# A hybrid encoder layer on one core: last projection granule and logits by token tile, a shorter reciprocal root, second low parts split around the first ranks, and the facts' casts on GpSimd

## The reference

```python
def prep(x, pos, g_norm1, w_in, b_forget, g_fox_q, g_fox_k, g_mem_q):
    h = rmsnorm(x, g_norm1)
    z = h @ w_in
    rq, rk, rv, rg, fq, fk, fv, ff, mq, gl = jnp.split(z, SPLIT_POINTS, axis=-1)
    fq = rmsnorm(heads(fq, H_F, D_F), g_fox_q)
    fk = rmsnorm(heads(fk, H_F, D_F), g_fox_k)
    mq = rmsnorm(heads(mq, H_M, D_M), g_mem_q)
    ...
def merge_and_ffn(...):
    merged = (gates[..., 0, :] * (o_r @ w_br_ret) + gates[..., 1, :] * (o_f @ w_br_fox)
              + gates[..., 2, :] * (o_m @ w_br_mem))
    x = x + merged @ w_out
    return x + hier_moe(rmsnorm(x, g_norm2), ...)
def hier_moe(h, w_rg, b_rg, w_re, b_re, w_g, w_u, w_d):
    lg = t @ w_rg + b_rg                        # 4 groups: the best one is taken
    le = t @ w_re + b_re                        # 8 experts of that group: the best two
    ...
    for g in range(N_GROUPS):                   # 32 experts, 1024 -> 256 -> 1024
        a = jnp.einsum('td,edf->tef', t, w_g[g]); u = jnp.einsum('td,edf->tef', t, w_u[g])
        out = out + jnp.einsum('tef,efd->td', jax.nn.silu(a) * u * comb[:, g, :, None], w_d[g])
```

## Time and profile before

| | |
|---|---|
| median of 3 runs | 659.27 us (658.0 to 659.7) |
| the profiled execution | 657.81 us |
| its span, first to last instruction | 656.0 us |
| PE busy | 630.8 us (96%) |
| DVE, ACT, POOL busy | 348.1, 255.8, 125.7 us |
| granted TensorE clock, mean | 0.998 |
| HBM | 167.48 MB read, 9.06 MB written |

### The profile page before, as it was taken

How to read it: one execution, slowest core, us unless ns; L and a number is a source line. 1 busy time by engine, 2 the same in 40 slices (tenths; PEclk the granted TensorE clock), 3 DMA queues, 4 the chain that set the end, 5 groups by cost and what they waited for, 6 DMA issues and landing times.

```text
span 656.0 us, 9434 instructions
## 1 busy us (share of the span) xinstructions
PE 630.8 (96%) x3509; PEld 422.0 (64%) x3509; DVE 348.1 (53%) x745; ACT 255.8 (39%) x487; POOL 125.7 (19%) x139
## 2 busy tenths in 40 slices
PE   5999999998999999999999999999999999999995
PEld 3887888877888776778777878763434444344431
DVE  4649347995357566744446855565533334234312
ACT  5673343346334455664953334332321222131200
POOL 0017525664000411010000010012301311210301
PEclk9999999999999999999999999999999999999999
DMA  8975432354222833203867989499999999999993
GB/s 304 423 272 186 146 130 92 125 204 182 78 84 97 295 131 129 98 33 129 325 223 291 427 321 373 142 386 351 425 428 424 428 426 425 425 425 428 427 419 116
DMA packets 36096, 176.67 MB, mean 269 GB/s; under 512 B 4256, under 2 KB 4528, under 8 KB 23632
## 3 DMA queue, kind: packets, MB, share of 16 engines
q1 hardware_dynamic: 33072, 164.87, 63.9%
q0 software_dynamic: 2976, 11.16, 4.8%
HBM read 167.48 MB, written 9.06 MB: 269 GB/s over the span
## 4 chain that ended last, share of the span: by engine, by line
PE 74%; issue 9%; SPq 5%; ACT 4%; DMA 4%; DVE 2%; POOL 0%; POOLq 0%; ACTq 0%; DVEq 0%
PE banks L1696 13%; PE banks L1698 13%; PE banks L1697 13%; PE banks L2070 12%; PE banks L2100 6%; SPq L836 5%; DMA piece<-in_wexp 4%; PE banks L2054 2%; PE banks L2110 1%; ACT z L1130 1%; PE banks L1899 1%; ACT w_hi L1010 1%; PE banks L1978 1%; PE banks L1865 1%; PE banks L1872 1%
## 5 line engine op out<-in xcount | busy, mean ns | idle before, releaser
L1250 DVE TENSOR_TENSOR w_lo<-raw,w_hi 128x1024 fp32r<-128x1024 f32 (+1 forms) x81 | 128.2, 1594 | 74.3 <-ACT w_hi L1010 71.2
L1696 PE MATMUL banks<-w_hi,hT_hi 128*128 128x512 f32 x312 | 124.7, 400 | 2.4 <-ACT z L1037 1.7
L1698 PE MATMUL banks<-w_hi,hT_lo 128*128 128x512 f32 x312 | 121.8, 391 | 0.0
L1697 PE MATMUL banks<-w_lo,hT_hi 128*128 128x512 f32 x312 | 121.6, 390 | 0.0
L1010 ACT ACTIVATE w_hi<-raw 128x1024 fp32r<-128x1024 f32 x79 | 83.5, 1057 | 90.8 <-PE banks L1698 87.1
L2070 PE MATMUL banks<-piece,xs 128*64 128x512 f32 x512 | 114.7, 593 | 0.5 <-DMA piece<-in_wexp 0.5
L2070 PEld LDWEIGHTS banks<-piece,xs 128*64 128x64 f32 x512 | 38.3, 137 | 72.8 <-issue 70.2
L1696 PEld LDWEIGHTS banks<-w_hi,hT_hi 128*128 128x128 f32 x312 | 58.6, 188 | 15.6 <-issue 2.9
L1698 PEld LDWEIGHTS banks<-w_hi,hT_lo 128*128 128x128 f32 x312 | 58.6, 188 | 12.7
L1697 PEld LDWEIGHTS banks<-w_lo,hT_hi 128*128 128x128 f32 x312 | 58.7, 188 | 11.3
L2100 PE MATMUL banks<-piece,act_T 128*64 128x512 f32 x256 | 58.5, 599 | 0.1
(11 more groups left out here) (353 smaller groups left out, 951.2 us busy)
## 6 DMA issues: line engine op xcount, KB each, us to landing
piece<-in_wexp SPq DMA_DIRECT2D x90, 1024.0 KB, 18.8
raw<-in_wstream SPq DMA_DIRECT2D x79, 512.0 KB, 4.3
piece<-in_wexp SPq DMA_DIRECT2D x12, 512.0 KB, 20.7
foxc<-in_foxc POOLq DMA_DIRECT2D x8, 512.0 KB, 4.5
memv<-in_memc SPq DMA_DIRECT2D x8, 512.0 KB, 5.8
memk<-in_memc SPq DMA_DIRECT2D x8, 512.0 KB, 5.9
xT<-in_xT SPq DMA_DIRECT2D x1, 1536.0 KB, 11.3
xtok<-in_xtok SPq DMA_DIRECT2D x1, 1536.0 KB, 7.9
```

The source lines that it names most:

```text
L1250: dve.tensor_tensor(w_lo[:, i % PART_SLOTS, cols], raw[:, i % RAW_SLOTS, cols], w_hi[:, i % PART_SLOTS, cols].bitcast(F32), ALU.subtract). ...
L1696: mm(out, xh, wh, start=start, stop=False, skip_group_check=True)
L1697: mm(out, xh, wl, start=False, stop=False, skip_group_check=True)
L1698: return mm(out, xl, wh, start=False, stop=stop, skip_group_check=True)
```

## The change

1. The last granule of the second output chunk runs tile by tile, 6 matmuls each: both halves `kk` of tile 0, then tile 1, then tile 2. Before, each half went over the three tiles.
2. Tiles 0 and 1 of the transposed `x2` are brought out first (128x256), and tile 2 separately from banks 0 and 1 (128x128). ACT squares tile 2 between the two. The second logits run over tiles 0 and 1 first, then tile 2.
3. `rsqrt` takes one step of a third-order form with 4 instructions and one Newton step of 3 in place of three Newton steps: 9 instructions in place of 11, at every call. `norm2` loses another one, since the squares are now scaled on ACT.
4. `second_low` is cut in two: `second_whole(t)` (the fp32 matmul) and `second_low(t)` (minus `x_hi`). `second_whole(1)` stands before the first ranks, and `second_whole(0)` no longer waits for `x_hi`.
5. The three instructions for the facts of token row and `rstd2` go from DVE's `route_group` to GpSimd.
6. On DVE the first `compact_low` stands after the slots and no longer before them.

```diff
     step("compact", 0, 1, 1)
+    plain("slots", 0)
     s.append(("compact_low", 0, 0, 0, None))
-    plain("slots", 0)
...
-            for step in range(3):
-                chain(dve.tensor_tensor(tmp, out, out, ALU.mult))
-                chain(dve.scalar_tensor_tensor(tmp, tmp, -0.5, x, ALU.mult, ALU.mult))
-                ins = dve.scalar_tensor_tensor(out, tmp, 1.5, out, ALU.add, ALU.mult)
-                if step < 2:
-                    chain(ins)
+            chain(dve.tensor_tensor(tmp, out, out, ALU.mult))
+            chain(dve.tensor_tensor(tmp, tmp, x, ALU.mult))
+            chain(dve.scalar_tensor_tensor(tmp, tmp, -10.0 / 3.0, tmp, ALU.add, ALU.mult))
+            chain(dve.scalar_tensor_tensor(out, tmp, 5.0, out, ALU.add, ALU.mult))
+            chain(dve.tensor_tensor(tmp, out, out, ALU.mult))
+            chain(dve.scalar_tensor_tensor(tmp, tmp, -0.5 * 0.375 ** 3, x, ALU.mult, ALU.mult))
+            ins = dve.scalar_tensor_tensor(out, tmp, 0.5625, out, ALU.add, ALU.mult)
             return ins
...
-            dve.wait_ge(x2t_lg_ready, KT + 1)
+            dve.wait_ge(x2t_lg_ready, KT + 5)
...
-            dve.tensor_copy(info_parts[:, :, 4, 0], cst2("token_row"))
-            chain(dve.tensor_copy(info_parts[:, :, 5, 0], rstd2))
-            dve.tensor_tensor(info_parts[:, :, 5, 1], rstd2, info_parts[:, :, 5, 0].bitcast(F32), ALU.subtract).then_inc(info_in, 1)
...
+        def last_turned(j):
+
+            return ps[:, j % 2, P * (j // 2 - 2):P * (j // 2 - 1)]
+
+        def squares(act, i, t):
+
+            act.wait_ge(x2_ready, T * i + t + 1)
+            if 3 * i + t:
+                act.wait_ge(ss2_ready, 3 * i + t)
+            act.activation(sq_scratch[:, :], x2[:, t, 512 * i:512 * i + 512], ACT.Square, scale=D ** -0.5, accum_out=ss2[:, 3 * i + t:3 * i + t + 1]).then_inc(ss2_ready, 1)
...
+                    for t in range(T - i):
+                        squares(act, i, t)
                 elif kind == "turn_x2":
+                    n = TOK - P * i
                     for j in range(4 * i + 1, 4 * i + 4, 2):
                         act.wait_ge(x2t_lg_ready, j + 1)
-                        act.activation(h2T[:, j, :], ps[:, TURN_BANK[j], 0:TOK], ACT.Copy, scale=gk[:, 16 + j:17 + j]).then_inc(x2t_odd, 1)
+                        act.activation(h2T[:, j, 0:n], ps[:, TURN_BANK[j], 0:n], ACT.Copy, scale=gk[:, 16 + j:17 + j]).then_inc(x2t_odd, 1)
+                    if i:
+                        squares(act, 1, T - 1)
+                        for j in (5, 7):
+                            act.wait_ge(x2t_lg_ready, KT + 4)
+                            act.activation(h2T[:, j, n:TOK], last_turned(j), ACT.Copy, scale=gk[:, 16 + j:17 + j]).then_inc(x2t_odd, 1)
...
+                    if i:
+                        for j in (4, 6):
+                            dve.wait_ge(x2t_lg_ready, KT + 3)
+                            dve.tensor_scalar(h2T[:, j, n:TOK], last_turned(j), gk[:, 16 + j:17 + j], None, ALU.mult).then_inc(x2t_even, 1)
                 elif kind == "norm2":
                     dve.wait_ge(ss2_ready, 2 * T)
-                    chain(dve.tensor_tensor(ss2[:, 0:T], ss2[:, 0:T], ss2[:, T:2 * T], ALU.add))
-                    chain(dve.tensor_scalar(ss2[:, 0:T], ss2[:, 0:T], 1.0 / D, EPS, ALU.mult, ALU.add))
+                    chain(dve.scalar_tensor_tensor(ss2[:, 0:T], ss2[:, 0:T], EPS, ss2[:, T:2 * T], ALU.add, ALU.add))
...
+                elif kind == "route":
+                    pool.wait_ge(rstd2_ready, 1)
+                    pool.tensor_copy(info_parts[:, :, 4, 0], cst2("token_row"))
+                    chain(pool.tensor_copy(info_parts[:, :, 5, 0], rstd2))
+                    pool.tensor_tensor(info_parts[:, :, 5, 1], rstd2, info_parts[:, :, 5, 0].bitcast(F32), ALU.subtract).then_inc(info_in, 1)
...
+            def second_whole(t):
+
+                pe.wait_ge(x2_ready, T + t + 1)
+                mm(ps[:, t, :], ident, x2[:, t, 512:1024], start=True, stop=False, skip_group_check=True)
+
             def second_low(t):
 
                 pe.wait_ge(xhi_ready, T + t + 1)
-                mm(ps[:, t, :], ident, x2[:, t, 512:1024], start=True, stop=False, skip_group_check=True)
                 mm(ps[:, t, :], neg_ident[:, :], x_hi[1][t][:, :], start=False, stop=True, skip_group_check=True).then_inc(xlo_psum, 1)
...
-                    for kk in ((0,) if kind == "k" else (1,)) if i in halved else range(2):
+                    halves = ((0,) if kind == "k" else (1,)) if i in halved else range(2)
+                    for kk, tiles in product(halves, (range(nt),)) if i < NGRAN - 1 else [(h, (t,)) for t in range(nt) for h in halves]:
...
+                                to = ps[:, TURN_BANK[j], t * P:(t + 1) * P] if t < T - 1 else last_turned(j)
+                                ins = nc.tensor.transpose(to, x2[:, t, j * P:(j + 1) * P], ident)
+                                if t:
                                     ins.then_inc(x2t_lg_ready, 1)
                 elif kind == "logits":
                     pe.wait_ge(s_route_in, 32)
-                    for k in range(4 * i, 4 * i + 4):
-                        pe.wait_ge(x2t_odd if k % 2 else x2t_even, k // 2 + 1)
-                        for t in range(T):
+                    for tiles in ((range(T),) if i == 0 else ((0, 1), (2,))):
+                        for k, t in product(range(4 * i, 4 * i + 4), tiles):
+                            pe.wait_ge(x2t_odd if k % 2 else x2t_even, k // 2 + (3 if i and t == T - 1 else 1))
...
                 elif kind == "x_parts" and i == 1:
+                    second_whole(0)
                     second_low(0)
                 elif kind == "route":
+                    second_whole(1)
                     token_ranks(0, 32, 4, [T * NR + 4 * t for t in range(T)])
                     second_low(1)
+                    second_whole(2)
                     second_low(2)
```

More of the change, by code:

```diff
@@ L20 @@
 from contextlib import ExitStack
+from itertools import product
 import numpy as np
@@ L1136, in _ @@
                     act.wait_ge(u_oe, NGROUP)
-                    for t in range(T):
-                        act.wait_ge(x2_ready, T * i + t + 1)
-                        if 3 * i + t:
-                            act.wait_ge(ss2_ready, 3 * i + t)
-                        act.activation(sq_scratch[:, :], x2[:, t, 512 * i:512 * i + 512], ACT.Square, accum_out=ss2[:, 3 * i + t:3 * i + t + 1]).then_inc(ss2_ready, 1)
+                    for t in range(T - i):
+                        squares(act, i, t)
                 elif kind == "turn_x2":
+                    n = TOK - P * i
                     for j in range(4 * i + 1, 4 * i + 4, 2):
                         act.wait_ge(x2t_lg_ready, j + 1)
-                        act.activation(h2T[:, j, :], ps[:, TURN_BANK[j], 0:TOK], ACT.Copy, scale=gk[:, 16 + j:17 + j]).then_inc(x2t_odd, 1)
+                        act.activation(h2T[:, j, 0:n], ps[:, TURN_BANK[j], 0:n], ACT.Copy, scale=gk[:, 16 + j:17 + j]).then_inc(x2t_odd, 1)
[4 more added lines that the diff above has]
+                            act.activation(h2T[:, j, n:TOK], last_turned(j), ACT.Copy, scale=gk[:, 16 + j:17 + j]).then_inc(x2t_odd, 1)
                 elif kind == "x_parts":
@@ L1380, in _ @@
                 elif kind == "turn_x2":
+                    n = TOK - P * i
                     for j in range(4 * i, 4 * i + 4, 2):
                         dve.wait_ge(x2t_lg_ready, j + 1)
-                        dve.tensor_scalar(h2T[:, j, :], ps[:, TURN_BANK[j], 0:TOK], gk[:, 16 + j:17 + j], None, ALU.mult).then_inc(x2t_even, 1)
+                        dve.tensor_scalar(h2T[:, j, 0:n], ps[:, TURN_BANK[j], 0:n], gk[:, 16 + j:17 + j], None, ALU.mult).then_inc(x2t_even, 1)
+                    if i:
+                        for j in (4, 6):
+                            dve.wait_ge(x2t_lg_ready, KT + 3)
+                            dve.tensor_scalar(h2T[:, j, n:TOK], last_turned(j), gk[:, 16 + j:17 + j], None, ALU.mult).then_inc(x2t_even, 1)
                 elif kind == "norm2":
                     dve.wait_ge(ss2_ready, 2 * T)
-                    chain(dve.tensor_tensor(ss2[:, 0:T], ss2[:, 0:T], ss2[:, T:2 * T], ALU.add))
-                    chain(dve.tensor_scalar(ss2[:, 0:T], ss2[:, 0:T], 1.0 / D, EPS, ALU.mult, ALU.add))
+                    chain(dve.scalar_tensor_tensor(ss2[:, 0:T], ss2[:, 0:T], EPS, ss2[:, T:2 * T], ALU.add, ALU.add))
                     rsqrt(dve, chain, rstd2, ss2[:, 0:T], T).then_inc(rstd2_ready, 1)
@@ L1739, in _ @@
                         cols = slice(512 * kk, 512 * kk + 512)
-                        for t in range(nt):
+                        for t in tiles:
                             tok = slice(t * P, t * P + P)
```

2 lines of the change are left out of this document (removed).

## The result

The kernel after took 654.62 us (median of 4, 654.53 to 655.07), the one before 659.49 beside it: ratio 0.9931, interval 0.9913 to 0.9948. In two later comparisons after had 654.82 and 654.79 (ratios 0.9945 and 0.9939, that is 3.6 and 4.0 us less, where the first two medians are 4.9 apart).

The account below looks back on a forecast made before the run. The stream of weight pieces and PE were both taken as nearly the bound, so both must start earlier. Gains of 1.4 before the add and 1.2 in routing, 2.6 us, gave 656.7 against the median 659.27, range 655.3 to 659.2.

Parts of the forecast that it names:

- the base of 659.27: Median of the runs of before, from which the 2.6 us gain was taken to forecast 656.7.
- Roots before the add: Shorter roots bring the third add of `residual 1` 1.4 us sooner, bounds 0.2 and 1.5.
- the two places: PE's waits at 53.12 (0.62 us, for a `w_lo`) and 154.59 (0.83, for `z`): gains 0.6 and 0.8.
- Rival (1): Early part doesn't carry, as DVE and GpSimd waits hang on who starts first: 657.9 us, chance 0.18.
- From the add to the first `gu`: Routing part, from the third add to the experts: first `gu` 1.2 us sooner, bounds 0.3 and 1.8.
- if the stream's gaps stay: Sign of being wrong: gaps of the weight stream at 440 to 455 us, forecast 1.2 us smaller in sum, remain.
- (2): Routing part lost, to GpSimd's hold on DVE or the stream not using the earlier release: 657.6 us, chance 0.14.
- (3), late facts: Facts come late from GpSimd's three casts, so `info` waits for `info_in`: slower, 661.9 at 9 us of casts, chance 0.03.
- (4): Nothing at all, both the early and the routing part lost: 659.0 us, chance 0.05.
- The hold of GpSimd on DVE's best group: Three casts could hold DVE 0.3 us each, 0.9 in all, cutting the routing gain of 1.2 to 0.3; taken as 0.
- 0.60: Chance of the forecast itself, between 655.9 and 657.3 us, with a fifth of it at gains below 2.0.

Follow-up runs that it names:

- e1: The kernel before with the shorter root alone (seven calls, folded sum of `norm2`, scale in ACT's squares): median 656.42 us, ratio 0.9968 to before.
- e9: The kernel before with only the split low parts, the facts' casts on GpSimd and the first `compact_low` behind the slots: ratio 1.0 to before.
- e8: The kernel before with only the last granule, turns and logits by token tile: ratio 0.9998 to before.
- e15: The kernel before with the gates written to PSUM, from where DVE's copy and L1268's operation read them: ratio 0.9978 to before.

## Why the prediction missed

The direction and both mechanisms were right in the main; three sizes were not, and the second of them, the base of 659.27, took the largest part of the miss.

1. **Roots before the add, 1.4 us with a bound of 1.5: measured 2.05** (e1: 2.1). The term had the bracketed waits of PE for a bound, 0.62 and 0.83, and gave 0.6 and 0.8. PE's matmuls are in fact 0.83 sooner at 53.12, 1.08 at 126.93, 1.27 from 136.4 to the next wait, and 2.03 at 154.59: the two places give 0.83 and 0.76, and 0.44 comes between them. Brackets miss such time because the ends of the matmuls are modelled: one lasts 0.39 us on the page and the next starts after 0.23. At 53.12 the start before is at 52.11, 1.01 earlier, so that PE lost 0.78 and not 0.62. At 126.93 the start before is 0.42 earlier, the matmul's row shows no wait at all, and only the row of the weight load has it:

```profile
126.93 0.19 PEld L1696 LDWEIGHTS banks<-w_hi,hT_hi 128*128 128x128 f32 x1 [0.45 <-DVE w_lo L1250]
```

The chain of GpSimd carried more than the two roots that the term counted. The square for FK, before and then after:

```profile
117.63 2.75 POOL L1540 TENSOR_TENSOR zq<-z 128x1536 f32<-128x1536 f32 x1 [0.94 <-ACT z L1037]
```

```profile
116.74 3.44 POOL L1557 TENSOR_TENSOR zq<-z 128x1536 f32<-128x1536 f32 x1 [1.38 <-ACT z L1047]
```

GpSimd's first multiplication for FQ comes 1.33 sooner (107.22 for 108.55), but this square only 0.89, with a longer wait for ACT. So FQ's root is lost there, as the prediction said. What it had not seen is the order: DVE's `w_lo` is now under way before the square starts, and is through at 117.57 in place of 121.46. The square takes 0.69 longer for it, but DVE's sum comes 1.16 sooner (120.22 for 121.38), 0.27 more than the square. With FK's and MQ's roots, 0.43 and 0.40, GpSimd is 2.02 sooner at L1543 for MQ. Rival (1) had named such a turn of order, as a loss. This split is read from the rows; no run separates it. L1268 was forecast at 1.3 us and took 1.98, since DVE arrived sooner as well; what counts is its end, forecast to be 1.4 sooner and 2.04 sooner in fact.

2. **"Against the median 659.27, 656.7".** I had the profiled execution of before 1.45 below the median and carried the 1.45 over to after. After's profiled execution is 0.09 below its median. Of the miss of 2.1, this is 1.4, and 0.7 is the sum itself (profiled, 655.2 forecast, 654.53 measured). Counted from 657.81, the prediction's gains of 0.5 to 3.3 give 654.5 to 657.3. Most of the 1.45 was the draw of three executions: the median of 115 is 658.3, only 0.5 above 657.81. What before has more of than after is the fall of the clock, in a third of its executions, and the trace, taken of one without it, can't show it. What there was to see were the two pauses of PE, 0.47 and 0.80 in the earlier trace rows. I had priced the second by its length alone.

3. **From the add to the first `gu`, 1.2 us: measured 1.03** (3.08 less 2.05). The steps inside came out close: L735 0.63 for 0.46, `info` 1.24 for 1.25 (3.29 less 2.05), pick matrix 0.80 (423.82 for 426.67, less 2.05) for 0.67. The first `gu` stands at 432.8 for a forecast of 433.3. The gaps of the stream shrank by 0.4 at most and not by 1.2, which the difference between two executions of before can hide; by the prediction's own sign ("if the stream's gaps stay") that counts against it. Counted in bytes from 410 to 460 us, the gain arrived all the same, as the gaps sit 3 us earlier.

Rivals: (1) fell with e1, (2) with the rows of after behind the add (1.03 us more); (3), late facts, fell with the cast rows, 0.6 us in all; (4) fell with the result. The hold of GpSimd on DVE's best group, the lower bound of 0.3 us, was not put to the test: the casts took 0.6 us in all and were through at 420.60, and the best group starts at 420.66 (L724 to L728, 0.17 us each, as before). Only L735 ran beside them, in 0.58 as before, and it reads PSUM. The chances don't add up as told either: 0.60 less a fifth, and a tenth of 0.37, are 0.52 for faster and not 0.56.

## What to carry to other kernels

A profile of one execution that lies well below the median of the runs is a sign that some executions have something else: compare the mean granted clock of each with its time before carrying the difference over. Where PE has several short pauses close together on the path that sets the end, price them by what the clock does and not by their length, fill them with work that is wanted anyway, and count the low executions of both kernels, since one profile can't show how often it happens. Measure PE's waits from start to start, or read the rows of the weight loads, where a matmul is late by less than its own length. When a small VectorE instruction lasts as long as GpSimd's beside it, let it read PSUM.

## What the runs showed of the hardware

- PE's granted clock stood at 0.50 for 3.4 us (e9, e8, e15) or 6.8 us (e1) behind pauses of 0.47 to 1.34 us. Kernels that keep the pause ahead of the logits, or one of 1.34 us before the ranks, fell in 1 to 8 of 12 executions (before 38 of 115), those with one pause of 0.48 to 0.8 us before the ranks in 1 of 23; behind one of 1.98 us it was 11 of 12.
- Between a matmul of 128x512 and the next lie 0.23 us, and its row on the page lasts 0.39: a wait in brackets is 0.16 us short (0.62 for 0.78 at 53.12), and one hardly longer than that shows nowhere but in the row of the weight load.
- A VectorE instruction of 24 elements a row took 2.78 us beside a GpSimd multiplication from SBUF to SBUF with one SBUF input or with two, and 0.17 us with a PSUM input.
- GpSimd's casts of 128x3 took 0.19 to 0.20 us, less than the 0.29 of the larger one in the earlier trace rows and a little more than DVE's take (0.16 to 0.17).
